# A fifth place for split expert weights, splits one quarter further ahead, and the silu table loaded ahead of the expert loop

## The reference, cut to what matters

```python
def swiglu(h, w_gate, w_up, w_down):
    return (jax.nn.silu(h @ w_gate) * (h @ w_up)) @ w_down

def moe_swiglu(h, router, e_gate, e_up, e_down):
    ...
    top_vals, top_idx = lax.top_k(logits, TOP_K)
    w = jax.nn.softmax(top_vals, axis=-1)
    gates = jnp.einsum("nk,nke->ne", w, jax.nn.one_hot(top_idx, N_EXPERTS, dtype=jnp.float32)).astype(h.dtype)
    out = jnp.zeros_like(xt)
    for e in range(N_EXPERTS):
        out = out + gates[:, e:e + 1] * swiglu(xt, e_gate[e], e_up[e], e_down[e])
    return out.reshape(b, s, d)
```

## Time and profile before

| what | value |
|---|---|
| median of 3 runs | 1494.33 us (1490.82 to 1495.06) |
| the profiled execution | 1492.38 us, span of its records 1490.4 us |
| TensorE matmul busy | 1395.8 us (94%) |
| VectorE busy | 1174.1 us (79%) |
| ScalarE busy | 1070.0 us (72%) |
| GpSimd busy | 119.4 us (8%) |
| moved | 429.52 MB, mean 288 GB/s over the span |
| mean granted TensorE clock | 0.977 |

### The profile page before, as it was taken

The page is one execution under the profiler, slowest core; times in us unless marked ns, Lnnn a source line. Parts: engine busy times, 40 slices in busy tenths (PEclk is TensorE's granted clock), DMA queues, the critical chain, the costliest instruction groups (busy, mean ns, idle before and its releaser), DMA issues.

```text
span 1490.4 us, 19309 instructions
## 1 busy us (share of the span) xinstructions
PE 1395.8 (94%) x6469; PEld 1135.6 (76%) x6469; DVE 1174.1 (79%) x1451; ACT 1070.0 (72%) x1372; POOL 119.4 (8%) x181
## 2 busy tenths in 40 slices
PE   6998999997698699999999999999999999999997
PEld 5857788887466588788878878878887887887885
DVE  4785445545694599889989989988988998998996
ACT  4595444446494488887787887888888788788786
POOL 0100000000340610000000000000000000000000
PEclk9999999999799699999999999999999999999998
DMA  9706453212807499999999999999999999999990
GB/s 343 274 11 226 171 204 133 81 44 73 308 2 268 155 347 383 365 361 383 370 359 370 388 355 364 392 351 366 383 384 352 371 377 355 371 386 352 370 364 14
DMA packets 133138, 429.52 MB, mean 288 GB/s; under 512 B 4146, under 2 KB 11485, under 8 KB 133101
## 3 DMA queue, kind: packets, MB, share of 16 engines
q1 hardware_dynamic: 127692, 416.85, 74.8%
q0 software_dynamic: 2624, 9.47, 2.7%
q10 hardware_dynamic: 2784, 2.72, 0.5%
HBM read 422.73 MB, written 6.29 MB: 288 GB/s over the span
## 4 chain that ended last, share of the span: by engine, by line
PE 78%; issue 8%; DVE 7%; ACT 5%; DMA 1%; POOL 0%; ACTq 0%; SPq 0%; DVEq 0%; POOLq 0%
PE bank L576 25%; PE bank L578 24%; PE bank L577 24%; PE bank L540 1%; DVE w_lo L1156 1%; ACT w_hi L783 1%; DMA ring<-in_ev_w_in_dram 1%; DVE w_lo L1226 1%; PE bank L639 1%; ACT h L813 1%; PE bank L667 1%; PE bank L505 1%; ACT gs L803 1%; PE bank L656 1%; ACT w_hi L844 0%
## 5 line engine op out<-in xcount | busy, mean ns | idle before, releaser
L1156 DVE TENSOR_TENSOR w_lo<-ring,w_hi 128x1024 fp32r<-128x1024 f32 x672 | 792.1, 1223 | 74.0 <-ACT w_hi L783 46.0
L783 ACT ACTIVATE w_hi<-ring 128x1024 fp32r<-128x1024 f32 x672 | 702.8, 1063 | 156.1 <-PE bank L578 155.9
L576 PE MATMUL bank<-w_hi,hT_hi 128*128 128x512 f32 (+2 forms) x1264 | 494.2, 391 | 29.8 <-DVE w_lo L1156 13.4
L577 PE MATMUL bank<-w_hi,hT_lo 128*128 128x512 f32 (+2 forms) x1264 | 487.8, 386 | 0.0
L578 PE MATMUL bank<-w_lo,hT_hi 128*128 128x512 f32 (+2 forms) x1264 | 487.6, 386 | 0.0
L576 PEld LDWEIGHTS bank<-w_hi,hT_hi 128*128 128x128 f32 x1264 | 239.4, 189 | 88.1 <-DVE w_lo L1156 22.9
L578 PEld LDWEIGHTS bank<-w_lo,hT_hi 128*128 128x128 f32 x1264 | 239.5, 189 | 47.6
L577 PEld LDWEIGHTS bank<-w_hi,hT_lo 128*128 128x128 f32 x1264 | 239.7, 190 | 44.5
L576 PE MATMUL bank<-w_hi,aT_hi 128*128 128x512 f32 x570 | 227.2, 399 | 10.0 <-issue 5.6
L1226 DVE TENSOR_TENSOR w_lo<-ring,w_hi 128x1024 fp32r<-128x1024 f32 (+3 forms) x124 | 146.2, 1191 | 107.3 <-ACT w_hi L844 107.2
L578 PE MATMUL bank<-w_lo,aT_hi 128*128 128x512 f32 x570 | 223.7, 392 | 0.0
(11 more groups left out here) (237 smaller groups left out, 825.3 us busy)
## 6 DMA issues: line engine op xcount, KB each, us to landing
ring<-in_od_e_gate_dram SPq DMA_DIRECT2D x57, 2048.0 KB, 9.8
ring<-in_od_e_up_dram SPq DMA_DIRECT2D x56, 2048.0 KB, 9.9
ring<-in_od_e_down_dram SPq DMA_DIRECT2D x56, 2048.0 KB, 10.0
ring<-in_ev_w_gate_dram SPq DMA_DIRECT2D x5, 2048.0 KB, 7.7
ring<-in_ev_w_up_dram SPq DMA_DIRECT2D x5, 2048.0 KB, 7.7
ring<-in_ev_w_down_dram SPq DMA_DIRECT2D x5, 2048.0 KB, 8.0
ring<-in_ev_w_in_dram SPq DMA_DIRECT2D x4, 2048.0 KB, 19.9
ring<-in_ev_w_out_dram SPq DMA_DIRECT2D x2, 2048.0 KB, 19.0
```

Of the source, the lines that this page charges most:

```text
L576: pe.matmul(dst, hi, whi, start=first, stop=False)
L577: pe.matmul(dst, lo, whi, start=False, stop=False)
L783: act.activation(w_hi[:, (NQ + q) % SPLITS, :], ring[:, i % RING, j * QUARTER:(j + 1) * QUARTER], ACT.Copy).then_inc(hi_ready, 1)
L1156: dve.tensor_tensor(w_lo[:, place, :], ring[:, i % RING, j * QUARTER:(j + 1) * QUARTER], w_hi[:, place, :].bitcast(F32), ALU.subtract).the ...
```

## The change

Three things change, all in the expert loop and at its entry.

1. **A fifth place.** `e_hi_at` and `e_lo_at` list five places for a split quarter: the four of `w_hi` and `w_lo`, and as number 4 the free columns 128 to 255 of `hT_hi` and `hT_lo`, eight runs of 128 words. `E_PLACES` says which quarter of a slot goes where: 0 to 4 in turn, once only 0 to 3, so that 84 quarters come out even. A quarter's split waits for the quarter that used its place last (`same_place_before`): five quarters before, four for quarters 39 to 42, nine for quarter 43. TensorE reads a half of a quarter as 4 x 128 words. 16 of the 84 quarters are in place 4.
2. **Four ahead.** Four quarters are split ahead of the loop (`AHEAD = 4`), and step n splits quarter n + 4.
3. **The table.** A silu of one word stands ahead of the loop.

```diff
+E_PLACES = 7 * (0, 1, 2, 3, 4) + (0, 1, 2, 3) + 9 * (0, 1, 2, 3, 4)
+AHEAD = 4
...
+def place_of(q):
+    return E_PLACES[q % len(E_PLACES)]
+
+def same_place_before(q):
+    return max(r for r in range(q - len(E_PLACES), q) if place_of(r) == place_of(q))
...
+        e_hi_at = [w_hi[:, p, :].rearrange("p (a n) -> p a n", a=8) for p in range(SPLITS)]
+        e_hi_at += [hT_hi[:, :, CAP:2 * CAP]]
+        e_lo_at = [w_lo[:, p, :].rearrange("p (a n) -> p a n", a=8) for p in range(SPLITS)]
+        e_lo_at += [hT_lo[:, :, CAP:2 * CAP]]
...
             def quarter(s, q):
-                place = (NQ + q) % SPLITS
                 pe.wait_ge(lo_ready, s * EQ + (NQ + q + 1))
                 for m in range(2):
-                    at = m * NW
-                    wh, wl = w_hi[:, place, at:at + NW], w_lo[:, place, at:at + NW]
+                    wh, wl = (at[place_of(q)][:, 4 * m:4 * m + 4, :] for at in (e_hi_at, e_lo_at))
...
+            act.activation(rt[:, 1:2], eps[:, 0:1], ACT.Silu)
             take_gathered(1)
-            for q in range(LEAD - 1):
-                if q == 0:
-                    act.wait_ge(arrived[0], 16 * (uses[0] + 1))
-                act.wait_ge(quarter_used, NQ + q - SPLITS + 1)
-                act.activation(w_hi[:, (NQ + q) % SPLITS, :], ring[:, 0, q * QUARTER:(q + 1) * QUARTER], ACT.Copy)\
+            act.wait_ge(quarter_used, NQ)
+            for q in range(AHEAD):
+                i, j = q // 4, q % 4
+                if j == 0:
+                    act.wait_ge(arrived[i], 16 * (uses[i] + 1))
+                act.activation(e_hi_at[q], eights(ring[:, i, j * QUARTER:(j + 1) * QUARTER]), ACT.Copy)\
                    .then_inc(hi_ready, 1)
...
-                    act.wait_ge(quarter_used, s * EQ + (NQ + q - SPLITS + 1))
-                    act.activation(w_hi[:, (NQ + q) % SPLITS, :], ring[:, i % RING, j * QUARTER:(j + 1) * QUARTER],
+                    act.wait_ge(quarter_used, s * EQ + (NQ + same_place_before(q) + 1))
+                    act.activation(e_hi_at[place_of(q)], eights(ring[:, i % RING, j * QUARTER:(j + 1) * QUARTER]),
                                    ACT.Copy).then_inc(hi_ready, 1)
...
-                        split(4 * i + j + LEAD - 1)
+                        split(4 * i + j + AHEAD)
```

More of the change, by code:

```diff
@@ L462, in _ @@
             slots = over + N_EXP
-            sp.wait_ge(lo_ready, slots * EQ + (NQ + 4 * (1 - RING)))
-            load(0, 0, *order[0])
+            for i in range((AHEAD + 3) // 4):
+                sp.wait_ge(lo_ready, slots * EQ + (NQ + 4 * (i + 1 - RING)))
+                load(0, i, *order[i])
             sp.wait_ge(x_stored, 16)
@@ L508, in turn_rows, with out @@
                         mm.then_inc(rows_turned, 1)
+            def out(b):
+                return bank[b][:, :].rearrange("p (a n) -> p a n", a=4)
             def quarter(s, q):
@@ L513, in quarter @@
                 j = q % 4
-                place = (NQ + q) % SPLITS
                 pe.wait_ge(lo_ready, s * EQ + (NQ + q + 1))
                 for m in range(2):
-                    at = m * NW
-                    wh, wl = w_hi[:, place, at:at + NW], w_lo[:, place, at:at + NW]
+                    wh, wl = (at[place_of(q)][:, 4 * m:4 * m + 4, :] for at in (e_hi_at, e_lo_at))
                     if kind == "down":
                         half = slice((4 * part + j) * P, (4 * part + j + 1) * P)
-                        mm = three(bank[4 + m][:, :], eT_hi[:, half], eT_lo[:, half], wh, wl,
+                        mm = three(out(4 + m), eT_hi[:, half], eT_lo[:, half], wh, wl,
                                    c == 0 and part == 0 and j == 0, c == NCH - 1 and j == 3)
@@ L525, in quarter @@
                         b = 2 * (kind == "up") + m * (CHUNKS[c] == 2)
-                        mm = three(bank[b][:, :], hT_hi[:, k, 0:CAP], hT_lo[:, k, 0:CAP], wh, wl,
+                        mm = three(out(b), hT_hi[:, k, 0:CAP], hT_lo[:, k, 0:CAP], wh, wl,
                                    k == 0, k == KD - 1)
@@ L740, in _, with eights @@
             experts_pe(pe, three, turn_norm)
+        def eights(ap):
+            return ap.rearrange("p (a n) -> p a n", a=8)
         def experts_act(act, norm):
@@ L1145, in experts_dve @@
             take_gathered(1)
-            for q in range(LEAD - 1):
+            for q in range(AHEAD):
+                i, j = q // 4, q % 4
                 dve.wait_ge(hi_ready, NQ + q + 1)
-                place = (NQ + q) % SPLITS
-                dve.tensor_tensor(w_lo[:, place, :], ring[:, 0, q * QUARTER:(q + 1) * QUARTER],
-                                  w_hi[:, place, :].bitcast(F32), ALU.subtract).then_inc(lo_ready, 1)
+                dve.tensor_tensor(e_lo_at[q], eights(ring[:, i, j * QUARTER:(j + 1) * QUARTER]),
+                                  e_hi_at[q].bitcast(F32), ALU.subtract).then_inc(lo_ready, 1)
             with dve.Fori(0, slots) as s:
@@ L1153, in split @@
                     i, j = q // 4, q % 4
-                    place = (NQ + q) % SPLITS
                     dve.wait_ge(hi_ready, s * EQ + (NQ + q + 1))
-                    dve.tensor_tensor(w_lo[:, place, :], ring[:, i % RING, j * QUARTER:(j + 1) * QUARTER],
-                                      w_hi[:, place, :].bitcast(F32), ALU.subtract).then_inc(lo_ready, 1)
+                    dve.tensor_tensor(e_lo_at[place_of(q)], eights(ring[:, i % RING, j * QUARTER:(j + 1) * QUARTER]),
+                                      e_hi_at[place_of(q)].bitcast(F32), ALU.subtract).then_inc(lo_ready, 1)
                 def turned(c):
```

## The result

The changed kernel takes 1472.49 us (median of 5 runs, 1470.22 to 1479.71) against 1494.33 (5 runs, 1490.82 to 1499.66): a ratio of 0.986 with a 95% interval of 0.983 to 0.989. It is faster by some 22 us.

The account below looks back on a forecast made before the run. The prediction took TensorE's even step, broken three times a slot by late splits, as the bound; 12.6 + 4.6 + 1.8 = 19.0 us off 1492.38 gave 1473.4, 1475.3 as a median, and it took 1474, range 1468 to 1482.

Parts of the forecast that it names:

- three pauses: Breaks in TensorE's even step in each slot before the change: 1.80 us, 0.58 us and 0.23 us.
- The slot's start: Quarter 3's split waits behind the old slot's closing work and a table load; 1.80 us goes, seven times: 12.6 us.
- each edit alone: At a slot's start, no load but three ahead leaves 0.40 us lost; four ahead with the load leaves 0.34.
- The first silu: A table load and silu delay quarter 11's split; the 0.58 us pause goes, eight times: 4.6 us.
- the first product: VectorE's product y and small work delay quarter 19's subtraction; the 0.23 us pause goes, eight times: 1.8 us.
- The pattern of the fifth place: Access to place 4 as eight runs of 128 words, expected to cost ScalarE, VectorE and TensorE nothing.
- The bound of 77 us: Upper cost if each of 768 TensorE matmuls reading place 4 paid 0.10 us; rival of a slower kernel, 1552 us, chance 0.04.
- The table loads: On ScalarE, the rows give 1.28 us per load; the Trainium skill adds a drain of 1.38, 2.66 in all.
- Transfers: Rival: DMA transfers bound the slots, which stay 121.85 us, with a time of 1492 to 1494; chance 0.05.
- The sum: Expert loop gains of 12.6 + 4.6 + 1.8 = 19.0 us, off the profiled execution's 1492.38 us: 1473.4.

Follow-up runs that it names:

- the kernel with the load alone: The kernel before plus only a one-word silu ahead of the loop, four places and three ahead: 1480.68 us against 1495.51, ratio 0.992.

## Why the prediction was right

- **What bounds the kernel.** TensorE's even step bounds a slot, and three pauses that a feeder's order made stood in it. All three are gone and no other engine's work came into their place. The prediction's count left out a fourth, in front of quarter 80, of 0.04 to 0.06 us and 0.10 for the step behind it; the change left it as it was, so it is in neither the sum nor the gain.
- **The slot's start.** 12.6 us for seven slots. The predicted margin of quarter 4 was 0.96 us and 0.86 was left: the first split begins 0.30 behind the copy of the gates, where the table load had begun 0.20 behind it. The head of the loop has one wait more there, since quarter 4 is the first of its piece (`arrived1` in the listing ahead); with three ahead and no load the split begins 0.22 behind. That the wait makes the difference was not tested by itself. That each edit alone would leave 0.40 and 0.34 was close too: 0.42 and 0.41 late, with 0.11 behind each.
- **The first silu and the first product.** 4.6 and 1.8 us. Both are gone, with 2.0 us left where quarter 12 is wanted and 1.3 at quarter 20, for which 1.1 was worked out.
- **The pattern of the fifth place.** Taken at nothing, and nothing it is on ScalarE and VectorE; on TensorE, for which there had been no row, steps of 0.2275 against 0.2270 us leave 0.4 us at most. The bound of 77 us was far out. The Trainium skill's rule, Advanced Engine Details and Errata, section Memory Cachelines, by which accesses that stay in a 16-byte line run at full performance, agrees with this: the three jumps between runs of 128 words don't show.
- **The table loads.** The rows were right: 1.28 us and what stands in front, and no drain, as the kernel with the load alone showed by the 0.42 us that it left. The kernel before shows it at the silu of the earlier trace rows too, where the load stands between two activations: 883.25 + 1.28 = 884.53, and the silu begins at 884.54.

```profile
884.54 1.09 ACT L803 ACTIVATE gs<-bank 128x512 f32<-128x512 f32 x2
```

- **Transfers.** Not the bound, with 7 to 9% of room. The DMA share of 1.00, which spoke for this rival, does not tell how near the ceiling is: it read 1.00 at 367 and at 379 GB/s, and 1.03 at 409, where the transfers did bound the kernel.
- **The sum.** 19.0 us were predicted. From the end of the first slot to the end of the last the profiles give 7 x 2.82 = 19.7, where the sum had 18.3; the first slot gives 0.3, where it had 0.8, since TensorE ran twelve of its first steps at 0.43 us (granted clock 0.50) and only nine before. That is 20.1 together, and the medians give 21.8 with an interval of 16 to 26. So a slot gained 0.2 us more than predicted and came out at 119.05, just under the 119.1 to 119.3 that were named. Most of that is known: behind a pause not one step is slow but several, by 0.005 to 0.01 us each. In the five middle slots 16 to 22 steps without a pause are over 0.233 us before and 9 to 16 after, and their mean fell from 0.2275 to 0.2272 us, some 0.15 us over a slot.

## What to carry to other kernels

Where one engine keeps an even pace and others feed it through a few places, write down for each interruption of the feeders when the next buffer is ready and when it is wanted; both come from one slot's timeline, and here they told each pause to 0.1 us. Depth of buffers and order of the feeder's program are two things. With the loads out of the loop a slot took 119.93 us with neither, 119.54 with the place alone, 121.25 with the order alone and 119.05 with both: a free place that the program reaches too late stays empty, and a program that runs ahead without the place puts its wait in front of something else, which here was worse than to leave the order alone. And look for table loads in a loop's instructions: here the table at hand on entry differed from the body's, each turn paid two loads, and one activation ahead of the loop took both out, which alone was worth 15 of 1495 us.

## What the runs showed of the hardware

- A DMA share of 1.00 is no sign of saturated queues: 367 GB/s and 379 both read 1.00. The most that this loop's transfers gave, with pieces of 2 MB from HBM, is 408 to 410 GB/s, at a share of 1.03.
- In the attention of layer 0 one stretch of 252 matmuls took 47.7 to 57.0 us in nine profiled executions, with a granted clock of 1.00 to 0.82. In the slowest it was 0.50, the 1.2 GHz level, from 80 to 90 us and 1.00 from 100 us on; in the fastest it was 1.00 throughout, and from 70 to 80 us TensorE was busy 8.0 us in both. Which level it gets there differs from one execution to the next; what decides it was not looked into and stays open.
- A table load is 1.28 us on ScalarE with 0.01 to 0.02 us between its end and the next activation, and no drain.
- ScalarE's head of a loop costs it 0.20 to 0.30 us between its last instruction and the first of the next turn.
